# The end of the hybrid mixer: stick mask added by TensorE, gate sigmoids and the first mix placed elsewhere, slab subtractions moved back

## What is computed

```python
y_sb = stick_breaking_attention(q, k, v) @ w_sb          # 6 heads of 64
y_dsa = dsa_attention(...) @ w_dsa                       # sparse attention, 6 heads
y_hg = (rms_norm(hgrn2(...)) * silu(hg)) @ w_hg          # recurrence, 4 heads
mixed = sigmoid(g_sb) * y_sb + sigmoid(g_dsa) * y_dsa + sigmoid(g_hg) * y_hg
return mixed @ w_out

# stick-breaking attention, for each block of 128 queries and the keys up to its end
past = s_pos < t_pos
log_1m = where(past, log_sigmoid(-z), 0)
later = cumsum(log_1m, reverse=True) - log_1m
a = exp(where(past, log_sigmoid(z) + later, -1e30))
out = a @ v
```

## Time and profile before

| | us |
|---|---|
| median of three runs | 2815.32 |
| lowest and highest | 2810.13, 2821.41 |
| profiled execution | 2810.61 |
| its span | 2808.7 |

### The profile page before, as it was taken

The page is one execution under the profiler, slowest core; times in us unless marked ns, Lnnn a source line. Parts: engine busy times, 40 slices in busy tenths (PEclk is TensorE's granted clock), DMA queues, the critical chain, the costliest instruction groups (busy, mean ns, idle before and its releaser), DMA issues.

```text
span 2808.7 us, 32629 instructions
## 1 busy us (share of the span) xinstructions
PE 2589.3 (92%) x13511; PEld 2173.6 (77%) x13511; DVE 1895.4 (67%) x1984; ACT 1459.3 (52%) x1341; POOL 0.2 (0%) x4
## 2 busy tenths in 40 slices
PE   7988998987999999999999898899779999977999
PEld 7857996956888888888888686787468988855898
DVE  7455456445988888888888686577555556865555
ACT  3433335443767676667667574545433435553432
POOL 0000000000000000000000000000000000000000
PEclk9999999967999999999999999999789999987999
DMA  7534764406999998999999792453125545511454
GB/s 229 180 105 150 222 194 136 165 16 244 363 323 371 326 367 325 352 343 353 342 345 350 266 364 87 137 160 113 61 97 165 188 141 163 165 60 60 158 187 135
DMA packets 301812, 597.59 MB, mean 213 GB/s; under 512 B 13553, under 2 KB 105953, under 8 KB 301665
## 3 DMA queue, kind: packets, MB, share of 16 engines
q1 hardware_dynamic: 301664, 595.50, 61.6%
HBM read 594.41 MB, written 1.05 MB: 212 GB/s over the span
## 4 chain that ended last, share of the span: by engine, by line
PE 80%; DVE 12%; ACT 4%; issue 2%; DMA 1%; SPq 0%; DVEq 0%; ACTq 0%
PE ps L211 78%; DVE ring_rounded L705 3%; ACT high_rounded L692 2%; DVE arena_rounded L1861 1%; PE ps L1609 1%; PE ps L1197 1%; DMA ring<-in_w_down_dense 1%; DVE arena L2316 0%; DVE h L855 0%; DVE arena L2450 0%; DVE ring_rounded L1861 0%; DVE arena_rounded L715 0%; DVE xT L642 0%; DVE xT_rounded L648 0%; ACT xT_high_rounded L617 0%
## 5 line engine op out<-in xcount | busy, mean ns | idle before, releaser
L211 PE MATMUL ps<-high_rounded,arena_rounded 128*128 128x512 f32 x2664 | 838.5, 396 | 31.2 <-DVE arena_rounded L715 18.7
L705 DVE TENSOR_TENSOR ring_rounded<-ring,high_rounded 128x2048 fp32r<-128x2048 f32 (+3 forms) x231 | 513.8, 2231 | 348.7 <-ACT high_rounded L692 347.9
L692 ACT ACTIVATE high_rounded<-ring 128x2048 fp32r<-128x2048 f32 (+3 forms) x231 | 430.3, 1864 | 402.7 <-PE ps L211 387.7
L211 PEld LDWEIGHTS ps<-high_rounded,arena_rounded 128*128 128x128 f32 x2664 | 501.0, 191 | 138.2 <-DVE arena_rounded L715 21.8
L211 PE MATMUL ps<-ring_rounded,arena_rounded 128*128 128x512 f32 x1000 | 396.6, 397 | 0.0
L211 PE MATMUL ps<-xT_high_rounded,high_rounded 128*128 128x256 f32 x1280 | 365.3, 285 | 24.8 <-DVE xT_rounded L648 11.1
L211 PE MATMUL ps<-xT_high_rounded,ring_rounded 128*128 128x256 f32 x1280 | 363.5, 284 | 0.0
L211 PE MATMUL ps<-xT_rounded,high_rounded 128*128 128x256 f32 x1280 | 363.3, 284 | 0.0
L211 PE MATMUL ps<-arena_rounded 128*128 128x512 f32 x864 | 339.3, 393 | 0.0
L1861 DVE TENSOR_TENSOR arena_rounded<-arena,high_rounded 128x2048 fp32r<-128x2048 f32 x131 | 297.5, 2289 | 27.4 <-ACT high_rounded L1664 27.2
L1664 ACT ACTIVATE high_rounded<-arena 128x2048 fp32r<-128x2048 f32 x131 | 251.0, 1919 | 84.7 <-PE ps L211 83.2
(11 more groups left out here) (276 smaller groups left out, 3123.6 us busy)
## 6 DMA issues: line engine op xcount, KB each, us to landing
arena<-in_w_down_moe SPq DMA_DIRECT2D x76, 1024.0 KB, 5.3
arena<-in_w_up_moe SPq DMA_DIRECT2D x72, 1024.0 KB, 5.8
arena<-in_w_gate_moe SPq DMA_DIRECT2D x68, 1024.0 KB, 5.3
ring<-in_w_in SPq DMA_DIRECT2D x50, 1024.0 KB, 5.1
ring<-in_w_gate_moe SPq DMA_DIRECT2D x44, 1024.0 KB, 5.3
ring<-in_w_up_moe SPq DMA_DIRECT2D x40, 1024.0 KB, 5.7
ring<-in_w_down_moe SPq DMA_DIRECT2D x36, 1024.0 KB, 5.2
ring<-in_w_up SPq DMA_DIRECT2D x32, 1024.0 KB, 5.4
```

Source lines behind the costliest of these rows:

```text
L211: return self.pe.matmul(out, lhsT, rhs, start=start, stop=stop, skip_group_check=True)
L692: act.activation(as_rounded(m, m.highs[n % HIGHS][:, 0:size]), m.slots[n % RING][:, 0:size], ACT.Copy).then_inc(m.rounded, 1)
L705: dve.tensor_tensor(as_rounded(m, slot), slot, as_rounded(m, m.highs[n % HIGHS][:, 0:size]), ALU.subtract).then_inc(m.slabs_split, 1)
```

## The change

- **Mask on TensorE.** The stick scores get a function of their own, `tensor_stick_scores`: behind each of the two products a product of the identity and the 0 / -1e30 mask is accumulated on the diagonal block, one of 128 columns for each tile. `vector_stick` loses the multiplication and the addition on the diagonal blocks; its subtraction now raises the semaphore for ScalarE.
- **Sigmoids.** The two sigmoids leave `scalar_sticks` and stand in `scalar_attention` ahead of the third head's exponential.
- **First mix.** `pp` and `ppT` move from the place of `mixed` into the tile `xn`. VectorE mixes the recurrence's branch right behind the stick heads, waiting only for what was copied before the first turned head, and waits for the last stick output behind it.
- **Slab roundings and subtractions.** ScalarE's two in `scalar_sticks` (behind the logarithms and in turn 4) move to turns 2 and 5. VectorE's in `vector_stick` behind heads 1 and 4 become one behind head 3 and one behind the first mix. Ahead of the last mix one slab is subtracted instead of two, and behind the casts five instead of four.

```diff
--- before.py
+++ after.py
@@ -560,7 +560,7 @@
     m.zs = [a.take(384) for _ in range(HEADS_S)]
     m.ss = [a.take(384) for _ in range(HEADS_S)]
     m.cum = a.take(384)
-    a = Arena(m.arena, start - 2 * HEADS_H * S)
+    a = Arena(m.xn.rearrange("p t n -> p (t n)"))
     m.pp = [a.take(384) for _ in range(3)]
     m.ppT = [a.take(384) for _ in range(2)]
 
@@ -1187,6 +1187,19 @@
     bank = L.bank(ring)
     L.give_back(L.mm(bank[:, TILE_KEYS[0]], q[:, 0:P], k[:, 0:P]))
     L.mm(bank[:, TILE_KEYS[1]], q[:, P:S], k[:, 0:S]).then_inc(ring.full, L.up(ring.full))
+
+
+def tensor_stick_scores(pe, L, m, h):
+
+
+    rows = slice(DH * (h % 2), DH * (h % 2) + DH)
+    q, k = m.b_sqk[rows, h // 2, :], m.b_sqk[rows, 3 + h // 2, :]
+    pe.wait_ge(m.a.drained, L.room(m.a))
+    bank = L.bank(m.a)
+    L.give_back(L.mm(bank[:, TILE_KEYS[0]], q[:, 0:P], k[:, 0:P], True, False))
+    L.give_back(L.mm(bank[:, 0:P], m.ident, m.c("neg_strict"), False, True))
+    L.give_back(L.mm(bank[:, TILE_KEYS[1]], q[:, P:S], k[:, 0:S], True, False))
+    L.mm(bank[:, 2 * P:3 * P], m.ident, m.c("neg_strict"), False, True).then_inc(m.a.full, L.up(m.a.full))
 
 
 def tensor_turn_probs(pe, L, m, p):
@@ -2014,7 +2027,7 @@
                 else:
                     L.give_back(ins)
     for h in range(HEADS_S):
-        tensor_scores(pe, L, m, m.b_sqk[rows(h), h // 2, :], m.b_sqk[rows(h), 3 + h // 2, :], m.a)
+        tensor_stick_scores(pe, L, m, h)
         if h == 1:
             w = [L.slab("2.gate"), L.slab("2.gate")]
         if h % 2 and h // 2 < TT:
@@ -2120,18 +2133,15 @@
     act.wait_ge(m.scalar_step, L.at(m.scalar_step))
     for h in range(HEADS_S):
         act.activation(m.ss[h], m.ss[h], ACT.Ln, bias=1.0).then_inc(m.logf2, L.up(m.logf2))
-    scalar_split(act, L, m)
-    act.wait_ge(m.a.drained, L.at(m.a.drained))
-    for t in range(TT):
-        act.activation(m.b_gate[:, t, 0:2 * D], m.b_gate[:, t, 0:2 * D], ACT.Sigmoid).then_inc(
-            m.gates_ready, L.up(m.gates_ready))
+    gates_in = L.at(m.a.drained)
     for turn in range(HEADS_S + 2):
         if turn < HEADS_S:
             act.wait_ge(m.logits, L.next(m.logits))
             act.activation(m.pp[turn % 3], m.ss[turn], ACT.Exp).then_inc(m.sticks, L.up(m.sticks))
-        if turn == 4:
+        if turn in (2, 5):
             scalar_split(act, L, m)
         scalar_turned(act, L, m, turn + 1, HEADS_S, m.ppT, lambda h: m.b_o[:, 2 + h // 2, :])
+    return gates_in
 
 
 def scalar_mixer(act, L, m, layer):
@@ -2169,13 +2179,19 @@
     for t in range(TT):
         scalar_gate(act, L, m, GATE_ORDER[0], t, ACT.Sigmoid)
     scalar_levels(act, L, m)
-    scalar_sticks(act, L, m)
-
-    def split_ahead(turn):
+    gates_in = scalar_sticks(act, L, m)
+
+    def between(turn):
+        if turn == 2:
+
+            act.wait_ge(m.a.drained, gates_in)
+            for t in range(TT):
+                act.activation(m.b_gate[:, t, 0:2 * D], m.b_gate[:, t, 0:2 * D], ACT.Sigmoid).then_inc(
+                    m.gates_ready, L.up(m.gates_ready))
         if turn == 3:
             scalar_split(act, L, m)
 
-    scalar_attention(act, L, m, HEADS_D, m.d_s, m.d_p, m.d_pT, lambda h: m.b_o[:, 5 + h // 2, :], split_ahead)
+    scalar_attention(act, L, m, HEADS_D, m.d_s, m.d_p, m.d_pT, lambda h: m.b_o[:, 5 + h // 2, :], between)
     scalar_split(act, L, m, 2)
     for t in range(TT):
         for half in range(2):
@@ -2436,14 +2452,10 @@
 
 def vector_stick(dve, L, m):
 
-    both = lambda name: m.c(name).unsqueeze(1).broadcast_to([P, 2, P])
     for h in range(HEADS_S):
         dve.wait_ge(m.logf2, L.next(m.logf2))
         z, s = m.zs[h], m.ss[h]
         dve.scalar_tensor_tensor(s, z, 0.0, s, ALU.max, ALU.add).then_inc(m.vector_step, L.up(m.vector_step))
-        dve.wait_ge(m.vector_step, L.at(m.vector_step))
-        dve.tensor_tensor(on_diagonal(s), on_diagonal(s), both("before"), ALU.mult).then_inc(
-            m.vector_step, L.up(m.vector_step))
         dve.wait_ge(m.vector_step, L.at(m.vector_step))
         for t in range(TT):
             at = TILE_KEYS[t]
@@ -2451,11 +2463,8 @@
                                          s[:, at][:, ::-1], 0.0, ALU.mult, ALU.add)
         ins.then_inc(m.vector_step, L.up(m.vector_step))
         dve.wait_ge(m.vector_step, L.at(m.vector_step))
-        dve.tensor_tensor(s, z, m.cum, ALU.subtract).then_inc(m.vector_step, L.up(m.vector_step))
-        dve.wait_ge(m.vector_step, L.at(m.vector_step))
-        dve.tensor_tensor(on_diagonal(s), on_diagonal(s), both("neg_strict"), ALU.add).then_inc(
-            m.logits, L.up(m.logits))
-        if h in (1, 4):
+        dve.tensor_tensor(s, z, m.cum, ALU.subtract).then_inc(m.logits, L.up(m.logits))
+        if h == 3:
             vector_lows(dve, L, m)
 
 
@@ -2508,8 +2517,10 @@
     vector_lows(dve, L, m)
     vector_stick(dve, L, m)
     L.up(m.a.drained, 2 + 5 * 2 + 2 + HEADS_S + 2 * HEADS_S)
+    dve.wait_ge(m.a.drained, L.at(m.a.drained) - 2 * HEADS_S)
+    vector_mix(dve, L, m, 2, True)
+    vector_lows(dve, L, m)
     dve.wait_ge(m.a.drained, L.at(m.a.drained))
-    vector_mix(dve, L, m, 2, True)
     vector_split(dve, L, m, m.b_o[:, 2:5, :], m.o_high_sb)
 
     def lows_ahead(turn):
@@ -2522,7 +2533,7 @@
     L.up(m.a.drained, 2 * HEADS_D)
     dve.wait_ge(m.a.drained, L.at(m.a.drained))
     vector_split(dve, L, m, m.b_o[:, 5:8, :], m.o_high_dsa)
-    vector_lows(dve, L, m, 2)
+    vector_lows(dve, L, m)
     vector_mix(dve, L, m, 1, False, True)
     for t in range(TT):
         for half in range(2):
@@ -2534,7 +2545,7 @@
                 m.a.drained, 1)
         dve.wait_ge(m.a.drained, L.at(m.a.drained))
         dve.memset(m.small[:, 179 + t:180 + t], 0.0).then_inc(m.parted, L.up(m.parted))
-    vector_lows(dve, L, m, 4)
+    vector_lows(dve, L, m, 5)
     vector_add_acc(dve, L, m)
 
 
```

## The result

| | before | changed |
|---|---|---|
| median, us | 2813.99 (4 runs) | 2776.26 (4 runs, 2772.44 to 2780.19) |
| ratio | 1 | 0.9864, 95% interval 0.985 to 0.9877 |
| span of the profiled execution, us | 2808.7 | 2770.6 |

The change takes off 37.7 us, 1.36%. The forecast was 2787.5, and its range (2773 to 2803) holds the time, but its own case (2784 to 2791) doesn't: it missed a quarter of the gain.

The account below looks back on a forecast made before the run. The prediction took VectorE's six stick heads to hold nearly all of the 32.3 us stick stage. Gains of 10.2 and 3.7 us make 13.9 a layer, 27.8 in two: 2787.5 us from 2815.3, range 2773 to 2803.

Parts of the forecast that it names:

- Start of the sticks: First stick operation on VectorE: mask products at 0.56 us a head on TensorE delay it by 0.7 us.
- rival (c): Stick scores: mask products cost 1.12 us each, heads start 1 to 3 us a layer later; 2790 to 2796, chance 0.13.
- VectorE's heads, first exponential, tail: Stick stage: heads take 2.10 us, exponential no longer behind sigmoids, tail 7.5 us; parting 10.2 us earlier a layer.
- The rival of serial hand-overs: Stick heads: exponential, transposes, copies and values run one after another, 3.8 us a head; 2800.5 us, chance 0.12.
- Sigmoids hidden: Sparse attention: 6.3 us of table loads and sigmoids fit ScalarE's 10.60 us idle time; cost 0, 4.3 to spare.
- Subtractions moved back: Last mix: waits only for TensorE's bank 0 and starts 3.7 us earlier a layer; the later subtraction stays hidden.
- the clock's term: TensorE's products in the mixer's end: no gain from a higher clock counted; the rival put it at 5 us a layer.
- Rival (a): Sticks' sum and output product: TensorE's clock stays up, 3.0 and 2.0 us a layer; 2777.5 us, chance 0.22.
- the theory with the clock: In the experiments' expectations: the unforeseen 10 us came from TensorE's clock; 2761 and 2751 us for the last two kernels.

Follow-up runs that it names:

- run with the products alone: The kernel before with the mask products added on TensorE, VectorE's mask kept: 2812.48 us, ratio 0.9995.
- the kernels with the late rounding: The changed kernel with ScalarE's rounding of turn 5 moved behind the last stick output: 2773.25 us; with added unread TensorE products too: 2763.93 us.
- the idle products: The kernel before with 42 TensorE products a layer, whose result nobody reads, added in its gaps: 2799.28 us, ratio 0.995.
- the last two kernels: The changed kernel with late rounding and unread TensorE products, 2763.93 us; the same with the sparse attention's turn 3 slab work moved behind it, 2760.65 us.
- the mask last: The changed kernel compared with itself with the mask back on VectorE and no mask products: the latter 2789.46 us, ratio 0.9906.

## Why the prediction was right or wrong

**Start of the sticks: expected +0.7 us, measured -0.57.** Two errors of opposite sign. The price of a head's mask products was put at 0.56 us; they take 1.04, close to the 1.12 of rival (c): a head's scores went from 0.84 to 1.88 at full clock, each identity product 0.42. TensorE's rows of one head in the changed kernel, up to the start of the next:

```profile
1971.56 0.48 PE L211 MATMUL ps<-arena 64*128 64x128 f32 x2
1971.97 0.49 PE L211 MATMUL ps<-const 128*128 128x128 f32 x2
1972.39 0.70 PE L211 MATMUL ps<-arena 64*128 64x256 f32 x2
1973.02 0.49 PE L211 MATMUL ps<-const 128*128 128x128 f32 x2
1973.44 0.48 PE L211 MATMUL ps<-arena 64*128 64x128 f32 x2
```

Also both of the first two heads' products lie in front of the gate tile, not only head 0's: it starts 3.5 us behind the mark instead of 1.4. Against that the two gate tiles ran at full speed, which won 3.2 us (the half tile 4.54 to 2.95 us, the second tile 7.28 to 5.69). The run with the products alone shows that this outweighs them, 28.15 for 28.7.

**VectorE's heads, first exponential, tail: right.** The first exponential starts at 1991.53, 2.4 us behind the first stick operation (3.2 forecast). Stick heads of the changed kernel on VectorE, and the end of the stage:

```profile
1989.12 0.55 DVE L2458 SCALAR_TENSOR_TENSOR arena<-arena 128x384 f32<-128x384 f32 x1
1989.71 1.01 DVE L2462 TENSOR_TENSOR_SCAN arena<-arena 128x128 f32<-128x128 f32 x2
1990.75 0.56 DVE L2466 TENSOR_TENSOR arena<-arena 128x384 f32<-128x384 f32 x1
1991.23 0.55 DVE L2458 SCALAR_TENSOR_TENSOR arena<-arena 128x384 f32<-128x384 f32 x1
...
2002.88 2.47 DVE L2479 TENSOR_TENSOR arena<-ps,arena 128x512 f32<-128x512 f32 x4
2005.35 2.29 DVE L705 TENSOR_TENSOR ring_rounded<-ring,high_rounded 128x2048 fp32r<-128x2048 f32 x1
2010.63 0.56 DVE L713 CAST arena_rounded<-arena 128x768 fp32r<-128x768 f32 x1 [3.00 <-ACT arena L1270]
```

Heads stand 2.11 apart (2.10 forecast; 3.03 in the earlier trace rows). From the first head to the parting it is 21.5 us (21.4 forecast). The tail behind the last head is 7.7 (7.5), and 3.0 us stay to spare behind the hidden mix and subtraction (2.7); in the earlier trace rows the mix ran right before the parting. The rival of serial hand-overs is out.

**Sigmoids hidden: right.** ScalarE's rows in the sparse attention:

```profile
2014.86 1.28 ACT L2189 ACT_TABLE_LOAD   x1
2016.16 3.72 ACT L2189 ACTIVATE arena<-arena 128x2048 f32<-128x2048 f32 x2
2019.89 1.28 ACT L1252 ACT_TABLE_LOAD   x1
2024.48 0.40 ACT L1252 ACTIVATE arena<-arena,small 128x128 f32<-128x128 f32 x1 [3.30 <-DVE small L1290]
```

The load ran ahead of the wait, as in the earlier trace rows, and 3.3 us were to spare (2.2 in the second layer, 4.3 forecast), in place of the idle 10.60 of the earlier trace rows. The cover was thin: the kernels with the late rounding lost it. The drain that the Trainium skill ("ScalarE: Activation LUTs", What ACT_TABLE_LOAD costs) adds to a load isn't visible here either: the sigmoid starts 0.02 us behind the load's end, and 0.01 us separates its end from the next load.

**Subtractions moved back: right in its mechanism, too small.** VectorE's last mix in the changed kernel:

```profile
2044.71 2.29 DVE L705 TENSOR_TENSOR ring_rounded<-ring,high_rounded 128x2048 fp32r<-128x2048 f32 x1 [0.31 <-ACT high_rounded L692]
2051.03 0.69 DVE L2482 TENSOR_TENSOR arena<-ps,arena 128x512 f32<-128x512 f32 x1 [4.03 <-PE ps L211]
```

It is released by TensorE, as forecast, where the earlier trace rows show the rounding of a slab in front of it. It came 5.3 us earlier behind the parting, 13.49 to 8.19, not 3.7: the sparse sum in front ran at full clock, where 3.5 us of it had been low. With the undone subtractions the first layer lost 3.75. The moved subtraction wasn't late: TensorE's output product has no gap.

**The step that failed is the clock's term.** The forecast took 0 for it and had 5 us a layer as a rival with a chance of 0.22. Measured, by the stretches in which low time fell: 1.3 at the start of the sticks (against what was expected, the dearer products included), 1.0 and 3.5 in the two layers' sparse stretch, 1.6 ahead of the last mix, 1.2 in the output product; the two layers' marked stretches gained 5.0 and 7.4 us beyond the forecast's 13.9 each. That clock and time are tied so is shown by the idle products; how each of these terms divides between clock and wait is read from the low times and not tested one by one. The argument against the rival, that the clock had fallen in many gaps of this stretch, was true of the kernel before, whose gaps the change itself shortens. By what the Trainium skill ("TensorE: Matmul & The Clock Gate", HAM oscillation) says, gaps between bursts make each burst start slow; the forecast used this to deny the gain, but it speaks for one wherever a change shortens the gaps (here waits for ScalarE and VectorE, on the page waits for DMA), and the run with idle products agrees with it, by 14 us. It does stay erratic: the two layers of the changed kernel differ by 2.5 us in the sparse stretch with the same instructions.

**The rival's time was partly luck.** Rival (a) puts 3.0 us a layer in the sticks' sum, from its 15 slow products, and 2.0 in the output product. The idle products in the kernel before won just that in these places, 2.8 and 1.9. The change didn't: nine products of the first layer's sticks' sum still ran slow, it won 1.0 and 3.5 us there and 1.2 in the output product, and the rest came at the start of the sticks and ahead of the last mix, which (a) doesn't name. Also 2.2 us were lost outside the marked stretches. The upper bound of rival (c), 2796, doesn't follow from its 3 us a layer, which give 2793.5.

**What stays open.** Which gap will let the clock fall couldn't be told beforehand. The idle products were put into gaps seen in the traces, and the expectations of the theory with the clock for the last two kernels were off by 3 and 10 us; both had overlooked the wait for the table load. Why the part between the layers' marks takes 373.4 us in some kernels and 377.2 in others wasn't studied.

## What to carry to other kernels

Where TensorE alternates with other engines in short bursts, count its time at the lower clock as a term of its own, with the low time by stretch read from the granted clock, before and after; a wait removed there pays once for the wait and may pay again in the dense products behind it, and a wait added costs the same way (2.4 us of stall cost 5.6 to 6.7 a layer). Work moved to TensorE into its gaps can cost nothing (the mask products alone: ratio 0.9995). And parts that hand over to each other, as VectorE's mask and ScalarE's sigmoids do, can be worth less alone than together (7 to 8 us for the mask alone, 12 to 13 for the mask last), so neither an undone part nor a part alone gives its share of the whole. Last, work hidden in a wait has only the cover that it has: when the neighbour speeds up or the work starts later, as the sigmoids did by 2.7 us here, look again whether it is still hidden.

## What the runs showed of the hardware

Useless f32 products of 128 columns, 84 in the whole run, made a kernel 14 us faster. Two f32 products of 128 columns put between the score products of a head cost 1.04 us at full clock, nearly twice what the columns of the score products alone give (2.2 ns each); no run shows why. A table load of 1.28 us runs ahead of the wait of the operation behind it, but holds that operation up once the wait is shorter: by 1.3 us in three kernels. Exchanging only the place of one rounding and its subtraction made the stretch ahead of the last mix, with the same instructions, 1.9 us longer (8.19 to 10.08), at a mean clock of 0.71 instead of 1.00.
